# One decoder layer for a prompt and eight samples: nine gates ahead of the dilated branch, and cross-attention spread over the memory projection's slots

## The chip, the core and the metric

The kernel runs on one core of a Trainium2 chip. The metric is the device time of one launch in microseconds (us), lower is better; several executions are timed and their median is given. Beside the times there is a profile: one execution recorded instruction by instruction on each engine. The engines are called as the profile calls them: PE is TensorE's matmul, PEld its weight load, DVE is VectorE, ACT is ScalarE, POOL is GpSimd, SP is SyncE, which here only issues transfers.

## What is computed

A prompt of 256 rows and 8 samples of one row each go through one decoder layer that share every weight; the model width is 2048. The parts that the change touches:

```python
# token mixer: three branches on the same normalised input h
bd = einsum('btc,cd->btd', y_dil, w_br_dil)          # dilated attention, projected
merged = gate[0] * bp + gate[1] * bd + gate[2] * bg  # gates: sigmoid of columns of h @ w_in
y = einsum('btd,de->bte', merged, w_mix_out)
x = x + rmsnorm(y, n_mix_post)

# cross-attention, 4 heads of 256, 256 memory rows
q = einsum('btd,dn->btn', rmsnorm(x, n_x_pre), w_xq)
s = einsum('bthe,bmhe->bhtm', q, k) * 256 ** -0.5
o = einsum('bhtm,bmhe->bthe', softmax(s), v)
x = x + rmsnorm(einsum('btn,nd->btd', o, w_xo), n_x_post)
# prompt: k, v = rmsnorm(mem_prompt) @ w_xkv, which is an output too
# sample b: k, v come from cache_mem_kv[b], 256 rows x 4 heads x 256 each
```

All is float32. After cross-attention comes a gated MLP, which the change leaves as it is.

## The kernel before

**Slots.** Nearly all of the work is products of activations, held transposed (128 features x 264 columns, which are 256 prompt rows and 8 samples), with weight matrices that pass through the core once. A slot is 1 MB of weights: 128 columns of a matrix with 2048 rows, or, for the matrices with 1024 rows (`w_br_dil`, `w_br_pool`, `w_xo`), 256 columns, then called a pair, whose two output tiles go to two banks. Every weight is split into two float32r parts, and so is every activation: ACT writes `weights_hi` (L481), DVE writes `weights_lo` (L488), and PE does three matmuls for each 128x128 block, hi by hi, hi by lo and lo by hi (L511 to L513): 48 for a slot. The ring of weight slots has three places. SP loads the raw weights, ACT and DVE split the slot three ahead when a slot has been multiplied (`split_hi`, `split_lo`), and every engine walks the same list of slots in program order. Bank 0, 1 or 2 takes a slot's result; ACT or DVE evacuates it.

**Order.** Everything is written out by hand: each engine's program calls, slot by slot, its part of the product and then pieces of other work (`tail(j)`, `x_piece(p, h)`). A `Phase` gives slot numbers and banks, `Steps` numbers the semaphore events. Nothing is scheduled by a compiler, so an engine waits where its own program waits, and what is behind it waits too.

**The dilated branch.** The eight heads run in a loop of nine slots each (`dil_body`). What is left of a head (turning the probabilities, the samples' scores against the key cache, their softmax, the product with the value cache) is `dil_tail(k, h)`, with k from 0 to 8, placed one k behind each slot of the next head. After the last head four slots project gates (`pair_products`, `pair_gates`, `pair_sums`), with tail pieces 0 to 3 behind them; pieces 4 to 8 follow with no product between them. Then a loop does pairs of `w_br_dil` and gates, through a ring of four gates. The pool branch uses the same functions. The GLA branch ahead of them has ten gates first and then one branch slot and one gate in turn (`GB_SLOTS`).

**Mixer output, norm, memory.** `w_mix_out` takes 16 slots; DVE sums the squares. `norm(0, ...)` then computes the RMS norm, reads x again (turned by PE into banks 3 to 5 and read from there by DVE, L2353), sums the new squares on PE (L1734) and writes `h_hi` and `h_lo` in four groups. The memory was normed during `w_mix_out`. The 16 slots of `w_xkv` follow (keys first, then values): the first stands in the norm, and the norm's last part is laid between the next four. Each tile is copied to `mem_kv_tile` by ACT, turned by PE (`kv_turn`) and copied to `mem_kv_tokens` by DVE.

**Cross-attention.** The eight slots of `w_xq` come next, two for a head, and each head's attention is six pieces, one behind each slot from the second on (`X_ORDER`): scores and softmax of the prompt, spreading the sample's query over all partitions (L1772), products with the key cache on DVE (L2418), the samples' softmax, and the product with the value cache. That last one (L1834) is, for each sample, two halves of the head and two halves of the memory, a weight load of 128x128 of the cache and one moving column: 32 matmuls for a head. A head's pieces need 14 places, so six places have no slot. ACT issues the value cache's transfers (L1241), POOL the key cache's (L845), 8 of 256 KB for each head. `w_xo` follows with eight pairs, then the next norm and the MLP.

## Times and profile before

| | us |
|---|---|
| median of 3 runs | 2808.69 |
| lowest and highest | 2805.4 and 2809.19 |
| the profiled execution | 2803.14 |
| its span in the profile | 2801.6 |

| engine | busy us | share of the span |
|---|---|---|
| PE | 2673.8 | 95% |
| PEld | 2556.5 | 91% |
| DVE | 1549.1 | 55% |
| ACT | 1223.3 | 44% |
| POOL | 169.1 | 6% |

The page's second part shows the span in 40 slices; its row for PEclk is the clock granted to PE in tenths, and it is below 9 only in slices 26 to 28. A matmul's shown duration is longer than its share of the engine, since matmuls overlap: the distance between two starts is what one costs. Stretches below are in us from the span's start.

### The profile page before, as it was taken

How to read it: one execution, taken by the hardware profiler on the slowest of the kernel's cores; microseconds unless marked ns; L12 is line 12 of the kernel's file. 1: busy time of each engine (PE TensorE's matmuls, PEld its weight loads, DVE VectorE, ACT ScalarE, POOL GpSimd, SP SyncE). 2: the span in 40 equal slices, each digit the busy share in tenths (PEclk: the TensorE clock that was granted, in tenths of full speed). 3: DMA queues.
4: the chain of work that ended last, by engine and by line, in shares of the span. 5: the costliest groups of instructions: out<-in, count | busy, mean ns of one | idle time of the engine just before them, and what ended most of it. 6: DMA issues, size and time to landing. Idle time of an engine off the chain costs nothing. (4 is left out here: it accounts for less than half of the span.)

```text
span 2801.6 us, 53113 instructions
## 1 busy us (share of the span) xinstructions
PE 2673.8 (95%) x20951; PEld 2556.5 (91%) x20951; DVE 1549.1 (55%) x1937; ACT 1223.3 (44%) x1511; POOL 169.1 (6%) x270
## 2 busy tenths in 40 slices
PE   6799999999999999989999999998799999999997
PEld 5778878899999999979999889888799999999997
DVE  4455555444565555534654546442766665666666
ACT  4344444432444444434343534321555555444453
POOL 0020121000111111100000000120000000000000
PEclk9899999999999999989999999977899999999999
DMA  5686687766888888846666736753366666766564
GB/s 144 181 280 201 210 277 224 214 182 171 238 221 233 236 237 232 227 140 179 176 165 200 208 106 189 217 190 96 93 182 181 183 163 185 197 182 181 159 180 119
DMA packets 862672, 530.65 MB, mean 189 GB/s; under 512 B 13153, under 2 KB 842521, under 8 KB 861775
## 3 DMA queue, kind: packets, MB, share of 16 engines
q1 hardware_dynamic: 822583, 440.07, 57.5%
q0 software_dynamic: 23152, 74.95, 7.8%
q10 hardware_dynamic: 16832, 14.15, 1.6%
q8 instruction: 75, 1.23, 0.2%
q14 instruction: 30, 0.25, 0.0%
HBM read 499.79 MB, written 33.29 MB: 190 GB/s over the span
## 5 line engine op out<-in xcount | busy, mean ns | idle before, releaser
L511 PE MATMUL bank<-h_hi,weights_hi 128*128 128x264 f32 x4624 | 1333.4, 288 | 32.0 <-DVE weights_lo L488 14.4
L488 DVE TENSOR_TENSOR weights_lo<-weights_raw,weights_hi 128x2048 fp32r<-128x2048 f32 x407 | 932.1, 2291 | 771.3 <-ACT weights_hi L481 770.8
L512 PE MATMUL bank<-h_lo,weights_hi 128*128 128x264 f32 x4624 | 1316.1, 285 | 0.0
L513 PE MATMUL bank<-h_hi,weights_lo 128*128 128x264 f32 x4624 | 1314.5, 284 | 0.0
L511 PEld LDWEIGHTS bank<-h_hi,weights_hi 128*128 128x128 f32 x4624 | 877.2, 190 | 52.9 <-issue 29.6
L512 PEld LDWEIGHTS bank<-h_lo,weights_hi 128*128 128x128 f32 x4624 | 877.7, 190 | 2.0 <-issue 1.9
L513 PEld LDWEIGHTS bank<-h_hi,weights_lo 128*128 128x128 f32 x4624 | 872.9, 189 | 0.0
L481 ACT ACTIVATE weights_hi<-weights_raw 128x2048 fp32r<-128x2048 f32 x407 | 776.9, 1910 | 188.3 <-PE bank L513 186.2
L511 PE MATMUL bank<-y_hi,weights_hi 128*128 128x264 f32 x1232 | 352.9, 286 | 4.5 <-DVE y_lo L2280 3.8
L513 PE MATMUL bank<-y_hi,weights_lo 128*128 128x264 f32 x1232 | 351.7, 285 | 0.0
L512 PE MATMUL bank<-y_lo,weights_hi 128*128 128x264 f32 x1232 | 350.2, 284 | 0.0
L511 PEld LDWEIGHTS bank<-y_hi,weights_hi 128*128 128x128 f32 x1232 | 233.8, 190 | 5.1 <-DVE y_lo L2280 3.0
L513 PEld LDWEIGHTS bank<-y_hi,weights_lo 128*128 128x128 f32 x1232 | 233.9, 190 | 0.0
L512 PEld LDWEIGHTS bank<-y_lo,weights_hi 128*128 128x128 f32 x1232 | 233.9, 190 | 0.0
L1035 ACT ACTIVATE qkv<-bank 128x264 f32<-128x264 f32 x72 | 28.1, 390 | 257.3 <-PE bank L513 257.3
L511 PE MATMUL bank<-memory_normed_hi,weights_hi 128*128 128x256 f32 x256 | 73.9, 289 | 0.1
L512 PE MATMUL bank<-memory_normed_lo,weights_hi 128*128 128x256 f32 x256 | 72.7, 284 | 0.0
L513 PE MATMUL bank<-memory_normed_hi,weights_lo 128*128 128x256 f32 x256 | 72.5, 283 | 0.0
L1035 ACT ACTIVATE merged<-bank 128x264 f32 (+1 forms) x48 | 18.8, 392 | 105.8 <-PE bank L513 105.7
L1339 ACT ACTIVATE ffn_value<-bank,parameters 128x264 f32<-128x264 f32 x44 | 25.1, 571 | 90.0 <-PE bank L513 90.0
L1497 PE MATMUL bank<-gla_state_sample,gla_q_apart 128*8 128x512 f32 x128 | 58.2, 593 | 4.9 <-DVE gla_state_sample L2031 4.8
L1035 ACT ACTIVATE y_hi<-ffn_value 128x264 f32 (+1 forms) x44 | 18.7, 425 | 96.1 <-DVE ffn_value L2515 96.1
(353 smaller groups left out, 2251.9 us busy)
## 6 DMA issues: line engine op xcount, KB each, us to landing
weights_raw<-in_w_in SPq DMA_DIRECT2D x177, 1024.0 KB, 6.8
weights_raw<-in_w_up SPq DMA_DIRECT2D x88, 1024.0 KB, 5.8
weights_raw<-in_w_down SPq DMA_DIRECT2D x64, 704.0 KB, 4.8
gla_state_sample<-in_state_gla POOLq DMA_DIRECT2D x32, 512.0 KB, 6.1
out_gla_s<-gla_state_sample POOLq DMA_DIRECT2D x32, 512.0 KB, 6.3
weights_raw<-in_w_br_gla SPq DMA_DIRECT2D x16, 1024.0 KB, 6.0
weights_raw<-in_w_mix_out SPq DMA_DIRECT2D x16, 1024.0 KB, 6.1
weights_raw<-in_w_xkv SPq DMA_DIRECT2D x16, 1024.0 KB, 6.1
```

The source lines that it names most:

```text
L481: nc.scalar.activation(w_hi[:, r, :], raw[:, r, :], ACT.Copy).then_inc(hi_ready, 1)
L488: nc.vector.tensor_tensor(w_lo[:, r, :], raw[:, r, :], w_hi[:, r, :].bitcast(F32), ALU.subtract).then_inc(lo_ready, 1)
L511: nc.tensor.matmul(out, wh, xh, start=first and n == 0, stop=False)
L512: nc.tensor.matmul(out, wh, xl, start=False, stop=False)
L513: mm = nc.tensor.matmul(out, wl, xh, start=False, stop=last and n == len(blocks) - 1)
L1035: return nc.scalar.activation(out, in_, ACT.Copy)
L1339: nc.scalar.activation(c, bank[p.outs[j]][:, 0:T], ACT.Identity, scale=param(PC_CW + 176 + col, n), bias=param(PC_CB + col, n)).then_inc(S ...
L1497: mm = nc.tensor.matmul(bank[5][0:NS, :], g_qm[:, t, b, :], g_Ss[b % 4][:, t, :], start=b + t == 0, stop=b + t == NS)
```

## The change

Six things are altered.

1. **Dilated branch.** Nine gates (`DR`) are projected ahead of the branch, each behind it with one tail piece of the last head; then pairs of `w_br_dil` with up to two gates behind each (`DB_SLOTS`), nine places for gates and the banks in turn 0, 1, 2. The number of slots is the same.
2. **x read again.** The 16 turns of x move from the norm to behind four slots of `w_mix_out`; ACT and DVE copy them in turn to `x_residual`.
3. **Norm and projection order.** Three key tiles (`PH_KA`) stand in the norm, the sums of squares are laid between the blocks of the second; then come all eight slots of `w_xq`, the first of them waiting block by block for `h_lo`; then the other 13 slots of `w_xkv` (`PH_KB`).
4. **Attention in pieces.** `X_WORK` names the pieces behind each of slots 2 to 22 (slots 0 to 7 are queries, 8 to 20 memory tiles): `qs` query of the samples, `ka`/`kb` key cache, `sm` samples' softmax, `ps` its turn, `po`/`pv` product with the value cache, `sc`/`pt` prompt's scores and turn, `oo` prompt's output, `os` the samples' output. The first three half-pairs of `w_xo` multiply six of their eight blocks, those of the first three heads, ahead of the last head's output.
5. **Value cache product.** The samples' probabilities become the stationary operand (128x8, zero but for one column) and the cache moves in 256 columns: 16 matmuls for a head, written in four groups of 32 partitions of one bank, and two matmuls that sum the groups.
6. **Caches.** Three buffers take the four key and four value loads in turn (`X_LOADS`), all issued by POOL; the memory's rows are stored in three parts.

```diff
+        DR = 9
+        DB_SLOTS = []
+        for q in range(8):
+            DB_SLOTS.append(("pair", q))
+            DB_SLOTS += [("gate", n) for n in (DR + 2 * q, DR + 2 * q + 1) if n < KB]
-        PH_KV = Phase(book, 3, [1, 2, 0], 5)
-        PH_XQ = Phase(book, 8, [2, 0, 1, 2, 0, 1, 2, 0], 1)
+        KA = 3
+        PH_KA = Phase(book, KA, [1, 2, 0], 1)
+        PH_XQ = Phase(book, 8, [1, 2, 0, 1, 2, 0, 1, 2], 1)
+        PH_KB = Phase(book, KB - KA, ([0, 1, 2] * 5)[:KB - KA], 1)
...
-        X_ORDER = [[(s - 2 - 2 * h, h) for h in range(4) if 0 <= s - 2 - 2 * h < X_PIECES] for s in range(8 + X_PIECES)]
+        X_AGAIN = {(3, 1): range(0, 4), (3, 2): range(4, 8), (4, 0): range(8, 12), (4, 1): range(12, 16)}
+        X_WORK = {2: "qs0", 3: "ka0", 4: "kb0", 5: "sm0", 6: "ps0", 8: "po0 qs1", 9: "pv0", 10: "ka1 sc0",
+                  11: "kb1 qs2 pt0", 12: "sm1 ka2 sc1", 13: "kb2 ps1 pt1", 14: "po1 sm2", 15: "pv1 ps2", 16: "po2 qs3",
+                  17: "pv2 ka3 sc2", 18: "kb3 pt2 sc3", 19: "sm3 pt3 oo0 os0", 20: "ps3 oo1 os1", 21: "po3 oo2 os2",
+                  22: "pv3 oo3 os3"}
+        X_LOADS = [("k", 0, 0), ("v", 0, 0), ("k", 1, 1), ("k", 2, 2), ("v", 1, 0), ("v", 2, 1), ("k", 3, 2), ("v", 3, 0)]
...
             # PE, dilated branch
+            for j in range(DR):
+                product(pe, PH_DIL_G, j, j, 0, H_BLOCKS).then_inc(projected, 1)
+                dil_tail(j, 7, True)
+            pe.wait_ge(*V_DT.at("yls", 7))
...
             # PE, product with the value cache
-                    for b in range(NS):
-                        for t in range(2):
-                            c = 272 + t * NS + b
-                            for mt in range(2):
-                                mm = nc.tensor.matmul(bank[7][:, c:c + 1], vc2[:, b, mt, t * P:t * P + P],
-                                                      xps[:, mt, b:b + 1], start=mt == 0, stop=mt == 1)
+                    for b in range(NS):
+                        for mt in range(2):
+                            r = 32 * (2 * (b % 2) + mt)
+                            mm = nc.tensor.matmul(bank[3][r:r + NS, 0:NP], xps[:, mt, b, :], x_buffer("v", h)[:, b, mt, :],
+                                                  start=b < 2, stop=b >= NS - 2)
...
             # POOL, the caches
+            pool.wait_ge(*V_N[0].at("lo15"))
+            for half in range(2):
+                cache_load("k", 0, half)
+            for half in range(2):
+                pool.wait_ge(*V_X.at(f"k{4 * half + 3}_0"))
+                cache_load("v", 0, half)
+            pool.wait_ge(projected, PH_XQ.c(7) + 1)
+            for h in (1, 2):
+                for half in range(2):
+                    cache_load("k", h, half)
+            pool.wait_ge(*P_X.at("po_0"))
+            for half in range(2):
+                cache_load("v", 1, half)
```

ACT's program at the end of the last dilated head, before: a gate (L1107) and the split of the next weights (L481), then the tail's pieces 5 to 8.

```order
L1035 ACTIVATE y_hi<-bank 128x256
L1079 DMA k_cache<-in_cache_dil_kv 64x8x128
L1107 ACTIVATE gates_dil<-bank 128x264
L481 ACTIVATE weights_hi<-weights_raw 128x2048
L1082 ACT_TABLE_LOAD
L1082 ACTIVATE scores_sample,softmax_stats_sample<-scores_sample,softmax_stats_sample 8x323
L1035 ACTIVATE probs_sample_apart<-bank 128x2x8
L1035 ACTIVATE probs_sample_apart<-bank 64x8
L1035 ACTIVATE o_sample_tokens<-bank 8x128 x4
L1035 ACTIVATE y_hi<-bank 128x8
```

After:

```order
L1192 ACTIVATE gate_dil_127<-bank 128x264
L511 ACTIVATE weights_hi<-weights_raw 128x2048
L1192 ACTIVATE gate_dil_128<-bank 128x264
L511 ACTIVATE weights_hi<-weights_raw 128x2048
L1139 ACT_TABLE_LOAD
L1139 ACTIVATE scores_sample,softmax_stats_sample<-scores_sample,softmax_stats_sample 8x323
L1192 ACT_TABLE_LOAD
L1192 ACTIVATE gate_dil_129<-bank 128x264
L511 ACTIVATE weights_hi<-weights_raw 128x2048
L1092 ACTIVATE probs_sample_apart<-bank 128x2x8
L1092 ACTIVATE probs_sample_apart<-bank 64x8
L1192 ACTIVATE gate_dil_130<-bank 128x264
```

Between the exponential of the samples' scores and the copies of their probabilities there now stand a gate and a split.

DVE's program in the norm ahead of cross-attention, before, from the last scaled group of the mixer's output (`merged` by `rstd`) on:

```order
L2347 TENSOR_TENSOR merged<-merged,rstd 128x1056
L2353 SCALAR_TENSOR_TENSOR x_residual<-merged,parameters,bank 128x264 x4
L2338 TENSOR_SCALAR rstd<-bank 128x264
L2341 RECIPROCAL rstd<-rstd 128x264
L488 TENSOR_TENSOR weights_lo<-weights_raw,weights_hi 128x2048
L2388 COPY mem_k_a<-mem_kv_tile 128x256
L2369 TENSOR_TENSOR merged<-x_residual,rstd 128x1056
L2364 SCALAR_TENSOR_TENSOR h_lo<-merged,parameters,h_hi 128x264 x4
L488 TENSOR_TENSOR weights_lo<-weights_raw,weights_hi 128x2048
L2388 COPY mem_k_a<-mem_kv_tile 128x256
L2369 TENSOR_TENSOR merged<-x_residual,rstd 128x1056
```

After:

```order
L2489 TENSOR_TENSOR merged<-merged,rstd 128x1056
L2492 SCALAR_TENSOR_TENSOR x_residual<-merged,parameters,x_residual 128x264 x4
L518 TENSOR_TENSOR weights_lo<-weights_raw,weights_hi 128x2048
L2480 TENSOR_SCALAR rstd<-bank 128x264
L2483 RECIPROCAL rstd<-rstd 128x264
L2510 TENSOR_TENSOR merged<-x_residual,rstd 128x1056 x2
L2505 SCALAR_TENSOR_TENSOR h_lo<-merged,parameters,h_hi 128x264 x4
L2510 TENSOR_TENSOR merged<-x_residual,rstd 128x1056
L2505 SCALAR_TENSOR_TENSOR h_lo<-merged,parameters,h_hi 128x264 x4
L2510 TENSOR_TENSOR merged<-x_residual,rstd 128x1056
L2505 SCALAR_TENSOR_TENSOR h_lo<-merged,parameters,h_hi 128x264 x4
L518 TENSOR_TENSOR weights_lo<-weights_raw,weights_hi 128x2048
```

The split of a weight slot (L488, now L518) now stands ahead of the second root (`rstd<-bank`), x comes from `x_residual` in place of a bank, and the four groups of `h_lo` follow each other with one split among them, where a split, a copy and a scaled group stood between them.

PE's program at the last slots of cross-attention, before: the product with the value cache (L1834) and the next pieces follow each other without a slot.

```order
L513 MATMUL bank<-h_hi,weights_lo 128x264
L1834 MATMUL bank<-x_probs_sample,mem_v_cache 128x1 x32
L524 MATMUL bank<-identity,x_scores_sample_slots 8x128 x2
L524 MATMUL bank<-identity,x_probs 128x128 x4
L1772 MATMUL bank<-xq_sample_tokens,identity 128x256 x4
L1824 MATMUL bank<-identity,x_scores_sample 128x8 x2
L1808 MATMUL bank<-x_probs_turned,mem_kv_tokens 128x256 x4
L1772 MATMUL bank<-xq_sample_tokens,identity 128x256 x4
L1784 MATMUL bank<-mem_k_b,xq 128x256 x4
L524 MATMUL bank<-identity,xq 8x128 x2
```

After, from the end of the last memory slot's product on:

```order
L544 MATMUL bank<-memory_normed_hi,weights_lo 128x256
L557 MATMUL bank<-identity,mem_v_tile 128x128 x2
L1902 MATMUL bank<-identity,x_scores_sample 128x8 x2
L1931 MATMUL bank<-x_probs_turned_168,mem_kv_tokens 128x256 x4
L557 MATMUL bank<-identity,mem_v_tile 128x128 x2
L1913 MATMUL bank<-mem_cache_a,x_probs_sample_apart 8x256 x16
L1931 MATMUL bank<-x_probs_turned_169,mem_kv_tokens 128x256 x4
L542 MATMUL bank<-x_o_hi,weights_hi 128x264
L543 MATMUL bank<-x_o_lo,weights_hi 128x264
L544 MATMUL bank<-x_o_hi,weights_lo 128x264
```

The product with the last head's value cache has 16 matmuls of 256 columns, and the products of `w_xo` (`x_o_hi`) begin right behind the third head's output (`mem_kv_tokens`).

## Rows read from the trace of the kernel before

**Rows 1.** Table of stretches: stretch, us, busy PE, PEld, DVE, ACT, POOL, PEclk, DMA share, GB/s.
```profile
140.00:204.00 64.00, 62.63 (x435) 51.29 (x434) 33.38 (x45) 30.55 (x42) 12.95 (x19) 1.00 0.86 278
1172.00:1218.80 46.80, 34.21 (x289) 31.52 (x286) 24.25 (x37) 17.26 (x29) 7.43 (x14) 0.85 0.66 187
1652.80:1782.90 130.10, 118.58 (x890) 111.25 (x889) 73.90 (x86) 49.56 (x67) 7.26 (x10) 0.93 0.61 170
1782.90:1851.00 68.10, 68.10 (x491) 63.51 (x490) 34.12 (x92) 25.43 (x39) 11.51 (x16) 0.99 0.68 214
1851.00:1931.50 80.50, 71.63 (x321) 64.13 (x320) 20.09 (x88) 6.62 (x23) 7.51 (x10) 0.58 0.43 132
1931.50:1985.20 53.70, 50.73 (x402) 50.13 (x402) 25.30 (x25) 25.57 (x41) 0.00 (x0) 0.94 0.47 138
```

**Rows 2.** Timeline of PE, end of the last head's tail: start, us, instruction, idle before.
```profile
1205.82 0.78 PE L524 MATMUL bank<-identity,scores_sample_slots 128*8 128x128 f32 x3 [6.55 <-DVE scores_sample_slots L2099]
...
1218.82 0.58 PE L511 MATMUL bank<-y_hi,weights_hi 128*128 128x264 f32 x1 [0.78 <-DVE y_lo L2177]
...
1224.90 0.28 PE L511 MATMUL bank<-y_hi,weights_hi 128*128 128x264 f32 x1
1225.02 0.28 PE L512 MATMUL bank<-y_lo,weights_hi 128*128 128x264 f32 x1
```

**Rows 3.** Waits from 1165 to 1350 us: engine, line, releaser, total, times, longest.
```profile
PE bank L511 <- DVE gated_dil L2207: 3.0, 4, 0.8
```

**Rows 4.** Timeline of PE inside the loop over dilated heads.
```profile
1162.13 1.61 PE L1623 MATMUL bank<-v_cache,probs_sample_apart 128*8 128x128 f32 x48
```

**Rows 5.** Timeline of DVE, start of the norm ahead of cross-attention.
```profile
1655.69 0.42 DVE L2338 TENSOR_SCALAR rstd<-bank 128x264 f32<-128x264 f32 x1
```

**Rows 6.** Timeline of DVE, w_xo slots and the norm behind cross-attention.
```profile
1977.24 2.29 DVE L488 TENSOR_TENSOR weights_lo<-weights_raw,weights_hi 128x2048 fp32r<-128x2048 f32 x1 [1.36 <-ACT weights_hi L481]
...
1983.04 2.29 DVE L488 TENSOR_TENSOR weights_lo<-weights_raw,weights_hi 128x2048 fp32r<-128x2048 f32 x1 [1.36 <-ACT weights_hi L481]
1985.24 0.42 DVE L2338 TENSOR_SCALAR rstd<-bank 128x264 f32<-128x264 f32 x1
...
2001.10 0.43 DVE L2338 TENSOR_SCALAR rstd<-bank 128x264 f32<-128x264 f32 x1 [1.38 <-PE bank L1734]
...
2011.78 3.32 DVE L2364 SCALAR_TENSOR_TENSOR h_lo<-merged,parameters,h_hi 128x264 fp32r<-128x264 f32 x8
```

**Rows 7.** Timeline of PE, turns of x inside the first norm.
```profile
1658.38 0.38 PE L524 MATMUL bank<-identity,x_tokens_again 128*128 128x128 f32 x2
...
1658.85 0.44 PE L524 MATMUL bank<-identity,x_tokens_again 128*128 128x128 f32 x2
```

**Rows 8.** Timeline of PE, turns of two memory tiles, one slot apart.
```profile
1740.20 0.38 PE L524 MATMUL bank<-identity,mem_kv_tile 128*128 128x128 f32 x2
...
1746.08 0.38 PE L524 MATMUL bank<-identity,mem_kv_tile 128*128 128x128 f32 x2
```

**Rows 9.** Timeline of PE, attention pieces between two query slots.
```profile
1816.24 1.89 PE L1808 MATMUL bank<-x_probs_turned,mem_kv_tokens 128*128 128x256 f32 x8
1818.07 1.99 PE L1772 MATMUL bank<-xq_sample_tokens,identity 8*128 8x256 f32 x8
1819.98 1.99 PE L1784 MATMUL bank<-mem_k_a,xq 128*128 128x256 f32 x8
```

**Rows 10.** Groups by line, 1786 to 1931 us: count, busy us, mean ns, idle before.
```profile
L1834 PE MATMUL bank<-x_probs_sample,mem_v_cache 128*128 128x1 f32 x256 | 47.1, 320 | 2.3 <-DMA mem_v_cache<-in_cache_mem_kv 2.3
...
L2418 DVE CUSTOM_DVE_ANT_0 mem_k_cache<-mem_k_cache,bank 128x256 f32<-128x256 f32 x64 | 22.4, 410 | 0.1
```

**Rows 11.** DMA queues, 1690 to 1935 us: packets, MB, share of 16 engines.
```profile
q1 hardware_dynamic: 41843, 24.37, 35.7%
q0 software_dynamic: 3408, 11.57, 14.8%
```

**Rows 12.** Timeline of POOL: one head's keys are issued.
```profile
1775.94 5.78 POOL L845 DMA_DIRECT2D mem_k_cache<-in_cache_mem_kv  x8 [35.15 <-PE bank L513]
```


## What the change will do to the time

> **What bounds the kernel now.** I read the table of engines first: PE is busy 95% of the span, so there is little idle time to win, and the question is where PE's busy time is not worth its length. The 40 slices answer it: the granted clock is at full rate everywhere but in slices 26 to 28. The table of stretches puts figures on the places that the change touches [rows 1]: where the gates of the dilated branch begin PE is busy 34.2 of 46.8 us; in norm and memory slots 118.6 of 130.1; and in 1851 to 1931 it is busy 71.6 of 80.5 at a clock of 0.58, about half. By contrast 140 to 204 shows what the ring of weight slots can do: 62.6 of 64.0, clock 1.00, DMA engines busy 0.86. Then come timelines, for the price of each step, and the groups by line, where one product stands out: 256 matmuls of one column with 47.1 us [rows 10]. A slot costs 5.80 us with 264 columns [rows 6] and 5.88 with a memory tile and its turn [rows 8].
>
> The sums are made against the profiled execution, 2803.14; the median of the runs shown is 5.55 above it, and I add that at the end.
>
> **Dilated branch.** Today PE stands 6.55 for the samples' softmax [rows 2] and then needs 13.0 from 1205.82 to 1218.82 for three turns, the product with the value cache (1.54, by the distance of two starts in the loop [rows 4]), small turns: about 2.95 of work by the same rows, so 10.0 is lost. After it the clock is low: the pair's first 27 matmuls take 6.08, 0.225 each, until 1224.90, and 0.12 each from there [rows 2]; 27 x 0.12 is 3.3, so 2.7 are lost. Four waits for a bank behind a gate add 3.0 [rows 3]. Together 6.6 + 10.0 + 2.7 + 3.0 = 22.3. The change lays the last tail pieces behind gates, so all of it goes. What is late next: the softmax chain is 6.55 plus about 0.5 before PE stood, against a slot and the turns, 6.1, so 0.9 is left (bounds 0 and 6.55). And `y_lo` of the samples now stands on DVE behind a gate and a weight split, which waits for ACT: 0.42 by the same shape [rows 5] + 1.36 + 2.29 [rows 6] = 4.1 before the first pair, with 0.5 of low clock behind it. 22.3 − 0.9 − 4.1 − 0.5 = **16.8 gained**; 11 if the softmax stands whole, 22 if nothing does.
>
> **x read again.** Sixteen turns move into the mixer's output product, where PE has no idle time to hide them: two take 0.47 from start to start [rows 7] with others beside them, up to 0.5 each with its change of bank and operand, 16 x 0.5 = 8.0, and 0.3 for four restarts: **8.3 lost** there (4 if they cost 0.25 each). The copies lie beside slots of 5.80 on ACT and DVE, which are free there.
>
> **From the mixer's last sum to cross-attention's last sum.** The stretch lies between two like events, the first root on DVE at 1655.69 [rows 5] and at 1985.24 [rows 6]: 329.6 us. After the change:
> - Norm. The norm behind cross-attention already has the form that this one takes: from the first root to the second 15.9, to the end of the last `h_lo` 29.9, 1985.24 to 2015.1 [rows 6]. The new one has a split ahead of the second root, 1.36 + 2.29 = 3.7 [rows 6], and another between the groups, 2.2 beyond what hides it: 35.8. The first query slot is multiplied block by block behind `h_lo` and ends 0.4 later: 36.2. The three key slots in it cost nothing; they fill PE's idle time.
> - Seven query slots: 7 x 5.80 = 40.6 [rows 6].
> - Thirteen memory slots with their turns: 13 x 5.88 = 76.4 [rows 8]; the three tiles turned among the queries 0.8.
> - Attention, on PE. Each head has two spreads, the prompt's scores and its output, 1.9 each by the distance of starts [rows 9]: 7.6. Turns of scores, probabilities and queries are some 1.95 by rows of the same shapes [rows 7]. The new product with the value cache does not exist today. 16 matmuls of 256 columns are about 32 passes of 128; the 48 passes of [rows 4] take 1.54, so 1.0; but full float32 columns are half as fast in them if they are like the spreads, which gives 2.05. The bounds are 1.0 (groups of rows overlap) and 7 (they queue and each load shows); I take 2.05, since its 128x256 cache blocks are nearest to [rows 9]. 11.6 a head, 46.2 for four.
> - Its end: no product lies beside the last memory tile's turn and the last two output chains, copy and split, about 4.7 by [rows 6] (one split 2.29 and two copies of 0.42 with their hand-overs, twice less what overlaps).
> - Eight pairs of `w_xo`, 46.4, and 5.7 from the last product to the root, as before.
> - Stalls: clock 1, DVE 3 and DMA 2 = 6 (0 to 20).
>
> 36.2 + 40.6 + 76.4 + 0.8 + 46.2 + 4.7 + 46.4 + 5.7 + 6 = 263.0, against 329.6: 66.6 gained, with the 8.3 lost **58.3**. What goes is visible today: the 1-column product, whose 47.1 us [rows 10] run at half clock [rows 1], the six places without a slot, and the norm's idle time.
>
> Whether the cover is there. DVE has per slot a split of 2.29 [rows 6] and per head 16 key-cache products of 0.41, 64 with 22.4 us [rows 10]; halves of 2.8 lie behind different slots. The heaviest slot, the twelfth, has 10.2 on DVE against 9.9 on PE, so 1 to 3 us are late in all, the 3 above. DMA: eight cache loads are 16.8 MB, at 11.57 MB in 14.8% of 245 us [rows 11], or 319 GB/s alone, 53 us; 22 slots of weights at 279 GB/s by the other queue [rows 11] 79; the memory's rows 8. That is 140 of about 169 us, 0.83, and the stretch at 140 has 0.86 with PE busy [rows 1]. POOL takes 5.78 to issue a head's keys [rows 12], beside nothing that waits.
>
> Sum: 2803.14 − 16.8 − 58.3 = 2728.0, and with 5.55 the median is **2733**.
>
> **Rivals.**
> *The weights come late (B).* All eight cache loads now go through POOL, in bursts behind slots 8 to 13. If a burst takes two thirds of the DMA engines from the weights, a slot arrives every 11.3 us (1 MB at a third of 279 GB/s) where 8.6 us of PE work stand for one; 87 us of contention hold 7.7 such slots, 2.7 late each: 21 us, so 2754. For it: the engines would be 0.83 busy, with no room after a burst. Against it: in 1782.9 to 1851, with cache loads and weights together at 214 GB/s, PE is busy without a gap [rows 1]. The Trainium skill ("DMA: Bandwidth & Descriptors", section on queues, rings and completion order) has each DMA engine take its queues in turn, a packet at a time; by that the weights keep half, 7.5 us for a slot, and nothing would be late, as that stretch bears out.
>
> *The chains of the pieces wait (C).* Each piece hands over between PE, ACT and DVE, and behind both stand splits: today's split waits 1.36 for ACT [rows 6], and a piece that falls behind it comes 2.29 later. If in the 12 slots with two or more pieces PE stands 2 us for one of them, 24 us go: 2757. For it: the 4.1 before the first pair above is exactly this. Against it: the pieces are ordered so that a whole slot lies between two steps of a head.
>
> *The clock stays low (D), the slower side.* At 0.58 in 1851 to 1931 the same pieces run that are now spread over all slots [rows 1]: spreads with 8 rows, scores with 8 columns. If small operands among full products are enough to hold PE at 1.2 GHz (0.22 for a matmul instead of 0.12, as in [rows 2]), 13 x 48 matmuls cost 64 more and the pieces 35: 2832. It turns slower than before when about three quarters of the stage run at half clock. Against it: 1782.9 to 1851 has such spreads among slots and a clock of 0.99, and only the product with one moving column fills the low stretch [rows 1, 10]. The Trainium skill ("TensorE: Matmul & The Clock Gate", Part 1, on the clock gate) has the clock drop behind stretches in which the engine does little and come back with sustained matmuls; the rows agree, low under one-column matmuls and high under full slots, and by that D would not come.
>
> *The change does not do what it says (E).* Should the first query slot wait for all of `h_lo`, and the samples' last chain of the dilated branch stand idle at its new place, the norm keeps its 11.5 idle (130.1 − 118.6 [rows 1]) and the 16.8 are not gained: 28 back, 2761.
>
> **How the numbers follow.** My forecast 0.66, B 0.14, C 0.14, D 0.04, E 0.02. The forecast's own range: dilated part +6 to −5, turns −4, value-cache product −4 to +20, stalls −6 to +14; these rarely meet at one end, so 2713 to 2750. With B and C the range is **2713 to 2762**: it leaves out D and the high ends of B and C, under 2 in 10. The measurement tells this kernel from an unchanged one from about 0.2%, 6 us, on. All but D and a stray piece of the rest lie far below: faster 0.95, within it 0.01, slower 0.04.
>
> **What the profile after would show.** The slices' clock stays at 9 or more over cross-attention, and no stretch like 1851 to 1931 is left (D falls). Before the first pair of `w_br_dil` PE stands about 4 us for DVE. In the norm the first query's matmuls are released by `h_lo` one block at a time, and the three key slots lie in what was idle. The value cache's 16 matmuls of a head take about 2 us; 4 us or more would mean the groups queue. From the first root to the last sum it is about 263. If weights are late, `weights_hi` waits for DMA by more than 2 us in the slots from the eighth on (B); if chains are late, PE's waits in that stretch name DVE or ACT lines of the pieces and sum to over 15 (C). A stretch from root to root of over 290, or a mixer product longer by over 12, would make the forecast wrong.

## The result, and the profile of the changed kernel

| | before | changed |
|---|---|---|
| median | 2807.05 | 2733.17 |
| lowest and highest | 2805.2 to 2809.19 (4 runs) | 2728.69 to 2737.36 (4 runs) |
| profiled execution | 2803.14 | 2728.69 |

The ratio is 0.974, with a 95% interval of 0.9723 to 0.9758: 74 us faster, where 2733 was forecast. The changed kernel's page, parts 1 and 2 (the engines' busy time, and the clock in 40 slices):

```profile
span 2727.0 us, 52522 instructions
...
PE 2611.6 (96%) x20839; PEld 2495.9 (92%) x20839; DVE 1549.4 (57%) x1940; ACT 1225.0 (45%) x1534; POOL 193.3 (7%) x303
...
PEclk9899999999999999999999999999899999999998
```

PE is busy 62 us less than before, DVE and ACT no less. Of the clock's row the sections above tell too little: before it has 7, 7 and 8 from the 27th slice on, which they call 26 to 28, and an 8 in the second and the 18th as well. Now the 7s are gone, and there is an 8 in the second, the 29th and the last slice. The table of stretches over cross-attention, with the columns of [rows 1]:

```profile
1646.00:1683.00 37.00, 28.71 (x201) 26.61 (x200) 32.24 (x48) 20.50 (x40) 0.00 (x0) 1.00 0.22 62
1683.00:1735.70 52.70, 52.45 (x416) 50.75 (x414) 27.91 (x51) 19.86 (x21) 16.82 (x24) 1.00 0.93 276
1735.70:1863.10 127.40, 121.97 (x954) 109.09 (x952) 62.17 (x160) 45.45 (x84) 33.29 (x46) 0.97 0.75 232
1761.80:1767.80 6.00, 5.07 (x14) 3.17 (x15) 4.38 (x21) 2.33 (x6) 2.88 (x4) 0.60 0.88 253
1851.00:1910.00 59.00, 54.53 (x446) 52.08 (x438) 26.32 (x29) 28.68 (x50) 2.48 (x3) 1.00 0.64 179
```

No long stretch at a low clock is left, against 0.58 over 80.5 us before [rows 1]. The DMA engines are busy 0.93 in the query slots and 0.75 in the memory slots; one short stretch of 6 us has 0.60 and will be explained.

**The three terms.** Three marks part the program: the first turn of the memory's rows in the mixer's output product, the first root of the next norm, and the first root behind `w_xo`. The tile's rows on PE, of the kernel before and of the changed one (duration least, median, most; first and last start):

```profile
L524 PE MATMUL bank<-identity,memory_tokens x32: 272/421/477, 1598.9 to 1609.6; 128*128 128x128 f32 x32
```
```profile
L557 PE MATMUL bank<-identity,memory_tokens x32: 272/421/475, 1580.7 to 1591.4; 128*128 128x128 f32 x32
```

and the roots on DVE (timeline, changed kernel; the kernel before has them at 1655.69 [rows 5] and 1985.24 [rows 6]):

```profile
1646.04 0.43 DVE L2480 TENSOR_SCALAR rstd<-bank 128x264 f32<-128x264 f32 x1
```
```profile
1910.61 0.42 DVE L2480 TENSOR_SCALAR rstd<-bank 128x264 f32<-128x264 f32 x1
```

| | before | changed | gained | forecast |
|---|---|---|---|---|
| up to the memory's turns (dilated branch) | 1598.9 | 1580.7 | 18.2 | 16.8 |
| to the first root (turns of x) | 56.8 | 65.3 | −8.5 | −8.3 |
| to the root behind `w_xo` | 329.6 | 264.6 | 65.0 | 66.6 |

Together 74.7. **Dilated branch.** Timeline of PE at the last tail (before: [rows 2]):

```profile
1210.36 0.53 PE L557 MATMUL bank<-identity,scores_sample_slots 128*8 128x128 f32 x3
```
```profile
1217.38 0.81 PE L1692 MATMUL bank<-identity,scores_sample 8*128 8x8 f32 x6 [0.50 <-DVE scores_sample L2284]
...
1224.14 1.06 PE L1705 MATMUL bank<-v_cache,probs_sample_apart 128*8 128x128 f32 x32
```
```profile
1232.44 0.39 PE L1713 MATMUL bank<-sum_of_column_tiles,o_sample_tokens 128*128 128x8 f32 x2
1236.42 0.59 PE L542 MATMUL bank<-y_hi,weights_hi 128*128 128x264 f32 x1 [3.60 <-DVE y_lo L2293]
```

The turns wait for nothing, the turned scores 0.50 for the softmax and the first pair 3.60 for `y_lo`: 4.1 of idle where the prediction counted 16.6 as lost.

**Norm.** PE in the second half of the norm, the first query's products released by `h_lo` one group at a time (the two groups between wait 0.94 each):

```profile
1672.03 0.36 PE L542 MATMUL bank<-h_hi,weights_hi 128*128 128x264 f32 x1 [2.87 <-DVE h_lo L2505]
...
1681.33 0.39 PE L542 MATMUL bank<-h_hi,weights_hi 128*128 128x264 f32 x1 [1.97 <-DVE h_lo L2505]
...
1683.01 0.38 PE L557 MATMUL bank<-identity,mem_k_a 128*128 128x128 f32 x2
```

It ends at 1683.0, 37.0 behind the root, where 36.2 was forecast. **The new product** and the two waits that are left at the stage's end:

```profile
1735.77 1.91 PE L1913 MATMUL bank<-mem_cache_a,x_probs_sample_apart 128*8 128x256 f32 x32
```
```profile
1850.03 0.41 PE L557 MATMUL bank<-identity,mem_v_tile 128*128 128x128 f32 x2 [2.35 <-DVE mem_kv_tokens L2534]
...
1864.74 0.39 PE L542 MATMUL bank<-x_o_hi,weights_hi 128*128 128x264 f32 x1 [1.49 <-DVE x_o_lo L2590]
```

The product with a head's value cache takes 1.85, from 1735.77 to the next instruction at 1737.62 (2.05 forecast), where 47.1 went for four [rows 10]. **Late weights.** All waits from 1740 to 1770 us with DMA or PE, and the spreads behind them:

```profile
ACT weights_hi L511 <- DMA weights_raw<-in_w_xkv: 6.7, 1, 6.7
...
PE bank L557 <- DVE mem_kv_tokens L2534: 2.2, 1, 2.2
...
PE bank L1853 <- DVE x_scores_sample_slots L2545: 0.9, 1, 0.9
```
```profile
1763.14 3.77 PE L1853 MATMUL bank<-xq_sample_tokens,identity 8*128 8x256 f32 x8 [0.86 <-DVE x_scores_sample_slots L2545]
```

and from the view of the DMA engines, 1730 to 1780 us (busy tenths in 40 slices of that stretch), then 1731 to 1757 (queues with packets, MB and share of 16 engines; transfers of one tile, their count, KB each, median us from issue to landing), and SP's issue of one slot of weights:

```profile
DMA  9999999999999999999999899469996712899984
```
```profile
q0 software_dynamic: 2060, 6.81, 73.2%
q1 hardware_dynamic: 4533, 2.30, 32.3%
...
weights_raw<-in_w_xkv SPq DMA_DIRECT2D x3, 1024.0 KB, 19.8
```
```profile
1748.24 8.61 SPq L526 DMA_DIRECT2D weights_raw<-in_w_xkv  x1
```

The bursts for head 1's and 2's keys and head 1's values, eight transfers each, stand one behind the other from 1730 on, and the DMA engines are busy at nine tenths or more for 27 us. From 1731 to 1757 the caches have 73.2% of the engines' time and the weights 32.3% (the two overlap a little). The three slots of weights issued in that time land after 22.3, 19.8 and 15.3 us, where those just before and behind take 5.9, and SP's issue of two of them takes 5.76 and 8.61 us in place of 0.37. So ACT's split stands 6.7 us for one memory slot's weights. PE stands 3.0, and then eight passes of a spread take 3.7 us where 1.9 is their price [rows 9]: that is the short stretch with a clock of 0.60. Rival B happened, in one slot.

### The profile page after: what moved, and what is told of

The parts are those of the page before. It is cut to its first block and busy times, and to the rows that moved or that the text cites. A ratio compares the mean times of both kernels' runs of the same rounds, so it can differ in the third digit from the quotient of the medians.

```text
span 2727.0 us, 52522 instructions
## 1 busy us (share of the span) xinstructions
PE 2611.6 (96%) x20839; PEld 2495.9 (92%) x20839; DVE 1549.4 (57%) x1940; ACT 1225.0 (45%) x1534; POOL 193.3 (7%) x303
## 3 DMA queue, kind: packets, MB, share of 16 engines
q10 hardware_dynamic: 8128, 5.76, 0.7%
## 5 line engine op out<-in xcount | busy, mean ns | idle before, releaser
L518 DVE TENSOR_TENSOR weights_lo<-weights_raw,weights_hi 128x2048 fp32r<-128x2048 f32 x407 | 932.3, 2291 | 769.9 <-ACT weights_hi L511 769.1
L542 PEld LDWEIGHTS bank<-h_hi,weights_hi 128*128 128x128 f32 x4624 | 875.5, 189 | 57.3 <-issue 26.2
L1579 PE MATMUL bank<-gla_state_sample,gla_q_apart 128*8 128x512 f32 x128 | 58.2, 593 | 6.4 <-DVE gla_state_sample L2147 6.4
```

Of the source, the lines that this page charges most:

```text
L518: nc.vector.tensor_tensor(w_lo[:, r, :], raw[:, r, :], w_hi[:, r, :].bitcast(F32), ALU.subtract).then_inc(lo_ready, 1)
L542: nc.tensor.matmul(out, wh, xh, start=first and n == 0, stop=False)
L1579: mm = nc.tensor.matmul(bank[5][0:NS, :], g_qm[:, t, b, :], g_Ss[b % 4][:, t, :], start=b + t == 0, stop=b + t == NS)
```

## The experiments

The kernels ran in three groups, each on one chip with the kernel before beside it: `dil_only`, `x_only`, `one_column` and `no_product` (its median there 2807.60), `after_again`, `staggered`, `no_early` and `no_turns` (2805.92), and `six_times`, `form_old_order`, `three_moves` and `staggered_again` (2806.57). Every ratio is to the kernel before of the same group.

### Half of the change at a time

`dil_only` is the kernel before with part 1, `x_only` the changed kernel with part 1 undone. For `dil_only`, SP and PE (ACT and DVE in the same way); for `x_only` the same lines in reverse:

```diff
-            pair_branch_loads(PH_DIL_G, PH_DIL_B, PH_DIL_E, 1, A["w_br_dil"][0], dil_last)
+            for j in range(DR):
+                load(sp, PH_DIL_G, j, 0, gate_src(1, j))
+                dil_last(j)
...
-            pair_products(PH_DIL_G, PH_DIL_B, PH_DIL_E, y_hi, y_lo, lambda k: dil_tail(k, 7, True), [V_DT.at("yls", 7)])
+            for j in range(DR):
+                product(pe, PH_DIL_G, j, j, 0, H_BLOCKS).then_inc(projected, 1)
+                dil_tail(j, 7, True)
```

> The kernel before with the dilated part of the change alone (nine gates ahead, pairs with two gates behind). My theory: 16.8 us gained, so about 2790, with PE waiting about 4 us for y_lo before the first pair and no other idle time there. Rival: the waits only move (the softmax chain's 6.6 and the chain behind it reappear behind other gates), under 8 us gained, 2799 or more.

> The changed kernel with the dilated branch as before: parts 2 to 6 alone. My theory: 58 us gained against before, about 2749, and the gains of the two parts add up to the whole one within 3 us. Rival: the two parts share a gain through the clock or the DMA queues, and the sum differs from 74 by over 8.

Measured: `dil_only` 2789.74 (ratio 0.9939, 0.9922 to 0.9955), 17.9 gained for 16.8; `x_only` 2744.15 (0.9777, 0.9761 to 0.9793), 63.5 gained for 58.3. The tile's rows in `dil_only`, then the two roots on DVE in `x_only`:

```profile
L532 PE MATMUL bank<-identity,memory_tokens x32: 272/420/475, 1582.2 to 1592.9; 128*128 128x128 f32 x32
```
```profile
1662.73 0.42 DVE L2428 TENSOR_SCALAR rstd<-bank 128x264 f32<-128x264 f32 x1
```
```profile
1925.75 0.42 DVE L2428 TENSOR_SCALAR rstd<-bank 128x264 f32<-128x264 f32 x1
```

`dil_only` has the dilated part's 16.7 and the same 56.8 to the first root; its stretch from root to root, 332.7, is 3.1 longer than before, without a known reason. `x_only` takes 65.3 and 263.0, the sum of the forecast, and its longest wait of a split for weights is 1.0. By the medians the two halves make 81 and the whole 74, but each of these gains is uncertain by 4 to 5. In the profiles' stretches they add up: 16.7 − 8.5 + 66.6 = 74.8, against 74.7. That `x_only` has no late slot may be part of the difference of the medians; it is not shown.

### Late weights, early blocks, turns

`staggered`, on POOL:

```diff
             for h in (1, 2):
                 for half in range(2):
+                    if h + half > 1:
+                        pool.wait_ge(projected, PH_KB.c((0, 1, 2)[2 * h + half - 3] if h + half > 1 else 0) + 1)
                     cache_load("k", h, half)
...
             for half in range(2):
+                pool.wait_ge(projected, PH_KB.c(3 + half) + 1)
                 cache_load("v", 1, half)
```

`no_early`, on PE (the blocks stand in the pairs behind instead):

```diff
-                if u == X_EARLY:
-                    for j, r in ((0, 0), (0, 1), (1, 0)):
-                        xo_part(PH_XO, j, r, 0, 0, 6, each=lambda n: V_X.at(f"ols_{n // 2}"))
```

`no_turns`, on PE:

```diff
-                        for m in range(2):
-                            turn(out[:, m * P:m * P + P], xtok2[:, m, t * P:t * P + P], P)
```

> The changed kernel unaltered, as the measure for the three others of this chip. So far its runs lie near 2729 or near 2737; if the late weights of one slot are what parts them, about as many of each come again, median 2733.

> The changed kernel with three of the cache bursts on POOL spread out: the second half of head 1's keys waits for memory slot 8, head 2's keys for slots 9 and 10, head 1's values for slots 11 and 12. My theory: the 6.7 us that the weights of w_xkv come late in the changed kernel, and the low clock behind, cost it 6 to 8 us, which go: about 2726. Rival: the wait is an accident of that one execution, or comes back behind the later loads: within 2 us of the changed kernel.

> The changed kernel without the six early blocks of three half-pairs of w_xo: all of w_xo stands behind the last head's output. My theory: the 6.9 us that these blocks fill between the third output and the samples' sum stand empty, as the copies of four partition groups must end first, and the blocks' 6.5 are paid later: 5 to 7 slower, about 2739. Rival: the chain is short, PE waits 1 to 2 more: about 2735.

> The changed kernel without the 32 turns of the prompt's x behind the slots of w_mix_out; the 16 small ones of the samples stay (x is wrong from there on). My theory: PE has no idle time there, each pair costs 0.44, 7 us less: about 2726. Rival: they lie in gaps of PE and cost under 2 us.

| | median | range | root to root |
|---|---|---|---|
| after_again | 2733.73 | 2728.50 to 2739.55 | 269.1 |
| staggered | 2726.75 | 2723.54 to 2730.74 | 261.1 |
| no_early | 2731.50 | 2728.16 to 2734.48 | 269.2 |
| no_turns | 2727.24 | 2723.76 to 2728.83 | 268.8 |

`staggered` had 2727.15 in the third group. Waits of `staggered` and of `after_again`, 1680 to 1900 us:

```profile
PE bank L557 <- DVE mem_kv_tokens L2537: 2.3, 1, 2.3
...
PE bank L542 <- DVE h_lo L2508: 2.0, 1, 2.0
```
```profile
ACT weights_hi L511 <- DMA weights_raw<-in_w_xkv: 5.9, 1, 5.9
...
PE bank L557 <- DVE mem_kv_tokens L2534: 3.7, 2, 2.3
...
PE bank L1853 <- DVE x_scores_sample_slots L2545: 1.1, 2, 0.9
```

The late slot comes in both profiles of the changed kernel and in those of `no_early` and `no_turns` (6.7, 5.9, 6.5 and 5.8 us). `x_only` has the same bursts and the same shares of the DMA engines (72.8% and 30.8% over 26 us), and one split waits 1.0 there: the bursts are needed for the late slot, but what else decides is open. Of the profiles that spread them, `staggered` and `three_moves` have no such wait, and `staggered_again` has one of 2.5 behind a later burst; `one_column` and `six_times` below, whose longer product holds the third burst back by 5 us, have none. In `staggered` the weights have 58.2% and the caches 47.2% from 1733 to 1759, and the slots land after 6.3 to 7.2 us. Spreading gives 7.0 us by the medians of this group, and 3.5 and 8.0 by the two stretches of the changed kernel. The nine executions of the changed kernel have a median of 2733.7 and the ten of the spread one 2727.0; their ranges overlap, but in 79 of the 90 pairs of one with the other the spread one is faster, so the gain is real and its size uncertain. It is not what parts the runs near 2729 from those near 2737, as I had supposed: both profiles of the changed kernel have it. Their difference is 6.5 us that are there already at the first root (1652.5 for 1646.0), and 4.5 behind it; the granted clock is lower in several short stretches of the longer one, and why an execution gets more of these is open.

`no_turns` has 58.3 between its first two marks where the changed kernel has 65.3, so 32 turns cost 7.0, and 1.5 are left for the 16 small ones and what else moved: the turns lie on PE's path, as forecast. `no_early` is inconclusive: 2.2 faster than `after_again` by the medians, within both ranges, and its stretch of 269.2 lies with one of the changed kernel's two, 264.6 and 269.1. The 5 to 7 us that I gave the early blocks are not seen.

### Form and place of the product with the value cache

`one_column` has the old form at the new places; `six_times` has the new form six times over, as long as one column takes; `no_product` is the kernel before with 7 of 8 samples' products left out, and `form_old_order` is that with the new form for all eight samples ahead.

`one_column`, on PE:

```diff
                     for b in range(NS):
-                        for mt in range(2):
-                            r = 32 * (2 * (b % 2) + mt)
-                            mm = nc.tensor.matmul(bank[3][r:r + NS, 0:NP], xps[:, mt, b, :], x_buffer("v", h)[:, b, mt, :],
-                                                  start=b < 2, stop=b >= NS - 2)
+                        for t in range(2):
+                            c = 272 + t * NS + b
+                            for mt in range(2):
+                                mm = nc.tensor.matmul(bank[3][:, c:c + 1], x_buffer("v", h)[:, b, mt, t * P:t * P + P],
+                                                      xps[:, mt, b, b:b + 1], start=mt == 0, stop=mt == 1)
```

`six_times`, and `no_product`:

```diff
-                    for b in range(NS):
+                    for b in list(range(NS)) * 6:
```

```diff
-                    for b in range(NS):
+                    for b in range(1):
                         for t in range(2):
                             c = 272 + t * NS + b
```

`form_old_order` is `no_product` with this ahead:

```diff
+                    for b in range(NS):
+                        for mt in range(2):
+                            r = 32 * (2 * (b % 2) + mt)
+                            nc.tensor.matmul(bank[7][r:r + NS, 0:NP], xps[:, mt, :], vc2[:, b, mt, :],
+                                             start=b < 2, stop=b >= NS - 2)
```

> The changed kernel with the product with the value cache in its old form, one moving column each, at its new places behind the slots; the two matmuls that sum groups still run and their result is not used. My theory: among full slots the clock stays high, 64 passes of half of 0.18 us make 5.9 us a head in place of 1.8, so 16 us slower than the changed kernel, about 2749. Rival (D in small): the one-column form brings the low clock with it wherever it stands, 11.8 us a head and slots at half clock behind it, over 35 us slower, 2768 or more.

> The kernel before with 7 of 8 samples' products with the value cache left out (the samples' outputs of cross-attention are wrong). My theory: the one-column product is itself what the clock falls in, so 41 us of it go and the stretch behind runs near full clock, 10 to 20 us more: about 2750. Rival: the places without a slot hold the clock low whatever runs there; with the product gone the chains stand bare, the granted clock of 1851 to 1900 stays below 0.7 and 20 to 35 us are gained: 2772 to 2787.

> The changed kernel with each head's product with the value cache done six times (the same values), 11 us a head, as long as the one-column product takes in its place. If the one moving column is what the clock falls in, it stays up here: 5 x 1.84 x 4 = 37 us more, about 2770, granted clock above 0.95 in these stretches. Rival: any such long run of small products brings it down, with 8 stationary columns too: over 60 us more, 2795 or above.

> The kernel before with 16 matmuls of 256 moving columns in place of 7 of 8 samples' one-column products, at the old places (what they give is not used, and the samples' outputs are wrong). To be set against no_product, 2775. If order and form gain independently, the form is worth here what it is in the new order, 42 us: about 2765. If in the old order the chains and the value cache's transfers stand behind the product, it is worth no more than leaving the product out: 2775 to 2783.

| | median | ratio to before, interval | root to root | gained there |
|---|---|---|---|---|
| before | 2807.6 | | 329.6 | |
| no_product | 2775.31 | 0.9884, 0.9868 to 0.9901 | 302.9 | 26.7 |
| form_old_order | 2778.78 | 0.9898, 0.9883 to 0.9913 | 306.7 | 22.8 |
| one_column | 2771.33 | 0.9867, 0.9851 to 0.9884 | 307.0 | 22.5 |
| changed | 2733.17 | 0.974, 0.9723 to 0.9758 | 264.6 | 65.0 |
| six_times | 2764.23 | 0.9854, 0.9839 to 0.987 | 297.1 | 32.5 |

The head-0 product of `one_column` and of `six_times` on PE, and the table of stretches round it for each:

```profile
1737.10 10.97 PE L1914 MATMUL bank<-x_probs_sample_apart,mem_cache_a 128*128 128x1 f32 x64
```
```profile
1735.00:1750.00 15.00, 15.00 (x94) 14.92 (x93) 3.45 (x2) 3.98 (x7) 10.03 (x15) 0.67 1.03 332
```
```profile
1740.06 10.55 PE L1913 MATMUL bank<-mem_cache_a,x_probs_sample_apart 128*8 128x256 f32 x192
```
```profile
1735.00:1750.00 15.00, 15.00 (x229) 10.00 (x231) 4.59 (x2) 3.89 (x3) 11.28 (x16) 1.00 1.07 332
```

Both take 10.5 to 11 us on a PE that is busy throughout; under one the granted clock is 0.67, under the other 1.00. So my theory for `one_column` fell and its rival held: standing between full slots does not save it. It lost 38 us to the changed kernel, and its stretch is 42.4 longer: the four products take 10.83, 10.35, 11.26 and 11.66 us from first start to next instruction, 44.1 for 7.4, and 5.7 are left. Slots behind them at a low clock are in that (0.81 over the 8 us behind the second product). And it is the form, not the length, that the clock falls in: 192 passes of 256 columns, 55 ns each, run at full rate, and `six_times` has 32.5 us more from root to root, where its theory said 37. The form differs in two things, a 128x128 operand loaded for every column and a single moving column; which of them it is, no run separates. At full rate one column is no bargain either: in the second value product of `one_column`, begun at full clock, the first weight loads are 0.12 apart, more than the 0.09 that I took as half of the old ones:

```profile
1801.30 1.86 PEld L1914 LDWEIGHTS bank<-x_probs_sample_apart,mem_cache_a 128*128 128x128 f32 x16
```

In the old order the form gains little. Waits of PE from 1851 to 1925 in `no_product` and from 1786 to 1925 in `form_old_order`, and the stretch where the clock was low before:

```profile
PE bank L1834 <- DMA mem_v_cache<-in_cache_mem_kv: 10.7, 1, 10.7
PE bank L524 <- DVE x_o_lo L2463: 7.0, 3, 4.0
PE bank L1824 <- DVE x_scores_sample L2460: 3.6, 1, 3.6
```
```profile
1851.00:1900.00 49.00, 31.19 (x102) 23.22 (x102) 19.98 (x87) 7.74 (x22) 7.51 (x10) 0.62 0.72 212
```
```profile
PE bank L1824 <- DVE x_scores_sample L2465: 10.7, 2, 8.7
PE bank L524 <- DVE x_o_lo L2468: 3.1, 3, 2.0
PE bank L1833 <- DMA mem_v_cache<-in_cache_mem_kv: 1.9, 1, 1.9
```
```profile
1851.00:1900.00 49.00, 37.80 (x176) 25.15 (x168) 19.68 (x85) 6.34 (x19) 7.51 (x10) 0.64 0.60 186
```

With most of the product gone, PE waits for the next value cache (10.7) and for the chains (10.6), and the clock over 1851 to 1900 is 0.62, as it is in the kernel before: idle time has taken the product's place. With the new form in place it waits 8.7 once for the samples' softmax. Form and order thus gain 22.8 and 22.5 alone and 65.0 together: the places without a slot leave nothing to put into the time that the form frees, and slots do. `form_old_order` still holds one sample's old product, which costs about 6 by an eighth of the 47.1 of [rows 10]; with that added the form alone would gain some 29, still less than half. My theory for `no_product` (2750) fell, and its rival held, as did that for `form_old_order`.

### Three moves

Against `staggered`, on ACT (and the same on DVE), then on PE:

```diff
+                if j == DR - 1:
+                    dil_tail(j, 7)
                 split_hi(act, PH_DIL_G, j)
-                dil_tail(j, 7)
+                if j < DR - 1:
+                    dil_tail(j, 7)
...
-                elif u - 8 == KB - KA:
-                    kv_turn(KB - 1)
                 for w, h in work:
                     x_piece(w, h)
+                    if (w, h) == ("po", 3):
+                        kv_turn(KB - 1)
```

> The staggered kernel with two more moves: behind the ninth gate the last piece of the dilated tail stands ahead of the weight split on ACT and DVE, not behind it; and the last memory tile's turn on PE stands behind the last product with the value cache, not ahead of it. My theory: the 3.6 us that PE waits for y_lo fall to about 1.5, and the 2.35 in which it waits for the copy of mem_kv_tokens are filled: 4 us less than staggered, about 2723. Rival: another step of the same chains is as late, no difference to staggered (2727).

> The staggered kernel once more, beside three_moves on the same chip: 2727 as before, within 2 us.

Measured: `three_moves` 2719.76 (0.9689, 0.9676 to 0.9702), `staggered_again` 2727.15 (0.9719, 0.9706 to 0.9733): 7.4 faster, where 4 was expected, and faster than both kernels of the case. The first pair on PE, and the roots:

```profile
1232.37 0.39 PE L542 MATMUL bank<-y_hi,weights_hi 128*128 128x264 f32 x1 [0.47 <-DVE y_lo L2299]
```
```profile
1640.96 0.42 DVE L2489 TENSOR_SCALAR rstd<-bank 128x264 f32<-128x264 f32 x1
```
```profile
1901.72 0.42 DVE L2489 TENSOR_SCALAR rstd<-bank 128x264 f32<-128x264 f32 x1
```

The wait for `y_lo` is 0.5, not 3.6. The stretch of 10 us behind it tells why that gives more than 3.1 (`staggered_again`, then `three_moves`):

```profile
1236.00:1246.00 10.00, 8.17 (x48) 8.17 (x49) 1.77 (x2) 0.00 (x0) 0.00 (x0) 0.66 0.41 112
```
```profile
1236.00:1246.00 10.00, 10.00 (x85) 10.00 (x84) 4.18 (x6) 3.62 (x3) 0.00 (x0) 1.00 0.60 159
```

The wait let the clock down to 0.66: 23 matmuls of the pair start 0.22 apart in `staggered_again`, 2.3 us. Without it the clock stays. The memory's turns come at 1576.2 for 1582.4, 6.2 us earlier, of which 3.1 and 2.3 are these; the other 0.8 is open. The move of the last turn takes PE's wait there from 2.35 to 0.50, but the stretch from root to root is 260.8 for 261.3.

## Why the prediction was right, and where it was off

- **What bounds it:** PE's busy time at half clock and places without slots. Right: the stretch went, and PE's busy time fell by 62 of the 74 us.
- **Dilated branch, 16.8:** 18.2 in the profile, 16.7 in `dil_only`, 17.9 by its median. The softmax was given 0.9 (0.50), the pair's wait 4.1 (3.60). The term for the clock behind it, 0.5, was mis-sized: in the profiled execution 19 matmuls of the pair start 0.22 apart, 1.9 us, and 23 of them in `staggered_again`, 2.3.
- **Turns, −8.3:** −8.5; 7.0 of it are the 32 large ones.
- **Norm 36.2:** 37.0. **Value-cache product 2.05 a head:** 1.85, by the nearest row, as chosen; the upper bound of 7 was not needed.
- **Root to root 263.0:** 264.6, 269.1 in the second profile, 263.0 in `x_only`. The 6 us of stalls were near as a sum in the first, and wrong inside: DMA was given 2, and bursts together cost 3.5 to 8 against spread ones.
- **Rival B** (0.14) came true in its mechanism, for a shorter time. It had a burst take two thirds of the DMA engines; the trace has 73.2% for the caches, and the weights' 2.30 MB in 26 us are 11.9 us for a slot, where the rival said 11.3. But that lasted 26 us and not 87, the slots already in the ring covered the rest, and one split was late: PE stood 3.0, and the price is 3.5 to 8, not 21. So the step that was wrong in the forecast is the half share, 7.5 us for a slot. The Trainium skill ("DMA: Bandwidth & Descriptors", queues, rings and completion order) has each DMA engine take its queues in turn, packet by packet. The trace does not bear out halves from that: in the 26 us the profile has 4533 packets of the weights' queue with 2.30 MB and 2060 of the caches' with 6.81 MB, so the packets are neither equal in number nor in size; whether turns of another size lie behind it is not shown. Nor did the stretch 1782.9 to 1851 before bear it out, as the prediction says: there the weights' queue had 41.1% and the caches' 26.2%, so the two were not both full.
- **Rival C** (0.14): PE's waits for DVE and ACT from query to `w_xo`, without those behind the late slot, are 4.1 us (0.25, 2.35 and 1.49), not 24.
- **Rival D** (0.04): the clock stayed at 0.97 in the memory slots. `one_column` shows that small operands among full slots do bring the clock down when 128x128 operands meet one moving column, and `six_times` that 8 stationary columns with 256 moving ones don't.
- That the sum's two halves are of form and of order was not asked in the prediction. The runs show that neither alone gives half.

The predicted number met the median to 0.2 us, and that is luck: the terms were off by 0.2 to 1.6, the medians of the changed kernel vary by 0.6 and its runs by 11, from 2728.5 to 2739.55.

## What to carry to other kernels

Where PE is busy at half clock, ask which instruction brings the clock down and put its large operand on the moving side; here the product with one moving column cost its own length and slowed slots behind it, between full slots too. Form and order belong together: a cheaper product pays only if something can follow it, so fill the places without weights first or at the same time. When transfers are bundled behind one event, compare the burst with the ring's depth, and do not count on half of the DMA engines for the weights: here they had a third, and moved a quarter of the bytes. Waits for later slots, added on the issuing queue, gave some 7 us here.

## What the runs showed of the hardware

- The granted clock fell under 64 passes with 128x128 stationary and one moving column each, on a PE without a gap, to 0.67 over 15 us that hold them (at full rate for the first 3 us, at 1.2 GHz from there); 192 passes with 128x8 stationary and 256 moving columns, as long, had 1.00.
- PE's wait of 3.6 us ahead of a pair was followed by 19 to 23 matmuls at 0.22 us each, 1.2 GHz; behind a wait of 0.5 they start 0.12 apart from the first on, 2.4 GHz.
- float32 with 8 stationary columns and 256 moving ones in four partition groups: 55 to 58 ns a pass.
- With three bursts of cache loads of 2 MB each queued beside the weights, the weights had 32.3% of the DMA engines' time and 2.30 of 9.14 MB over 26 us, and three 1 MB slots landed 22.3, 19.8 and 15.3 us after their issue, where 6.0 is the whole kernel's median for `w_xkv`; the issue itself took 5.76 and 8.61 us for two of them, in place of 0.37.
